# Borrowed homes for early weight splits, and half of a third group turned by VectorE

## The reference, cut to what matters

```
m = pool_conformer_mixer(rms(x, g), ...)    # stage 0: two matrices, depthwise convolution, pooling
x = x + rms(m, post_g)
x = x + rms(relu(rms(x, g) @ w1)**2 @ w2, post_g)      # stage 1: w1 2048 x 8192, w2 8192 x 2048
m = short_conv_mixer(rms(x, g), ...)        # stage 2: 2048 x 6144, a convolution of 3 taps, 2048 x 2048
x = x + rms(m, post_g)
x = x + rms(relu(rms(x, g) @ w1)**2 @ w2, post_g)      # stage 3: as stage 1
x = x + hybrid_layer(rms(x, g), ...)        # stage 4: attention, spatial gating, gates, output matrix
```

## Time and profile before

| | |
|---|---|
| median of 3 runs | 2675.39 us (2675.36 to 2675.88) |
| the profiled execution | 2675.7 us |
| its span | 2673.7 us |
| TensorE busy | 2668.5 us (100%) |
| VectorE busy | 1946.9 us (73%) |
| ScalarE busy | 1287.9 us (48%) |
| GpSimd busy | 286.2 us (11%) |
| mean DMA rate | 193 GB/s |
| the chain that ended last | TensorE 99% |

### The profile page before, as it was taken

One profiled execution on the slowest core, in us unless ns is written; L12 is line 12 of the kernel. 1 busy time (PEld: TensorE's weight loads), 2 busy tenths in 40 slices (PEclk: granted clock), 3 DMA queues, 4 the chain that ended last, 5 costly groups with the idle time before them and its releaser, 6 DMA issues.

```text
span 2673.7 us, 31093 instructions
## 1 busy us (share of the span) xinstructions
PE 2668.5 (100%) x11921; PEld 2210.5 (83%) x11921; DVE 1946.9 (73%) x2674; ACT 1287.9 (48%) x1625; POOL 286.2 (11%) x263
## 2 busy tenths in 40 slices
PE   9999999999999999999999999999999999999999
PEld 8888888888888888888888888888888888888887
DVE  6888867666766787776777676668668869985564
ACT  7775544444444454444544444344455545544442
POOL 4841100000000010000100000000011001000000
PEclk9999999999999999999999999999999999999999
DMA  7555655555655556555556655555555655565554
GB/s 258 188 173 190 210 199 189 189 189 190 207 186 191 202 185 210 192 199 193 187 190 205 204 188 183 196 189 193 192 184 188 212 174 175 177 215 189 189 189 157
DMA packets 268148, 515.57 MB, mean 193 GB/s; under 512 B 8498, under 2 KB 28260, under 8 KB 267492
## 3 DMA queue, kind: packets, MB, share of 16 engines
q1 hardware_dynamic: 267732, 513.34, 57.3%
q10 hardware_dynamic: 272, 0.26, 0.0%
HBM read 511.47 MB, written 2.10 MB: 192 GB/s over the span
## 4 chain that ended last, share of the span: by engine, by line
PE 99%; DVE 0%; DMA 0%; ACT 0%; issue 0%; SPq 0%; DVEq 0%; ACTq 0%
PE bank L833 32%; PE bank L835 32%; PE bank L834 32%; PE bank L884 0%; PE bank L901 0%; PE bank L1063 0%; DMA x_res<-in_x 0%; DVE w_lo L812 0%; DMA w_raw<-in_ab_w_in 0%; PE bank L1077 0%; DVE tap_product L2093 0%; DVE z L2081 0%; PE bank L1049 0%; PE bank L1086 0%; PE bank L1087 0%; PE bank L1024 0%
## 5 line engine op out<-in xcount | busy, mean ns | idle before, releaser
L812 DVE TENSOR_TENSOR w_lo<-w_raw,w_hi 128x1024 fp32r<-128x1024 f32 x950 | 1182.1, 1264 | 445.0 <-ACT w_hi L794 438.5
L794 ACT ACTIVATE w_hi<-w_raw 128x1024 fp32r<-128x1024 f32 x954 | 972.1, 1056 | 607.2 <-PE bank L835 415.8
L833 PE MATMUL bank<-w_hi,A_lo 128*128 128x512 f32 x2432 | 950.6, 391 | 0.1
L835 PE MATMUL bank<-w_hi,A_hi 128*128 128x512 f32 x2432 | 946.8, 389 | 0.0
L834 PE MATMUL bank<-w_lo,A_hi 128*128 128x512 f32 x2432 | 946.5, 389 | 0.0
L833 PE MATMUL bank<-w_hi,B_lo 128*128 128x512 f32 x1408 | 548.7, 390 | 0.0
L835 PE MATMUL bank<-w_hi,B_hi 128*128 128x512 f32 x1408 | 547.8, 389 | 0.0
L834 PE MATMUL bank<-w_lo,B_hi 128*128 128x512 f32 x1408 | 547.8, 389 | 0.0
L833 PEld LDWEIGHTS bank<-w_hi,A_lo 128*128 128x128 f32 x2432 | 456.6, 188 | 96.6 <-DVE w_lo L802 1.4
L835 PEld LDWEIGHTS bank<-w_hi,A_hi 128*128 128x128 f32 x2432 | 456.5, 188 | 95.3
L834 PEld LDWEIGHTS bank<-w_lo,A_hi 128*128 128x128 f32 x2432 | 456.7, 188 | 93.4
(11 more groups left out here) (181 smaller groups left out, 1020.9 us busy)
## 6 DMA issues: line engine op xcount, KB each, us to landing
w_raw<-in_ffn_w SPq DMA_DIRECT2D x256, 1024.0 KB, 5.2
w_raw<-in_w_in SPq DMA_DIRECT2D x88, 1024.0 KB, 5.0
w_raw<-in_sc_w_in SPq DMA_DIRECT2D x48, 1024.0 KB, 5.1
w_raw<-in_ab_w_out SPq DMA_DIRECT2D x16, 1024.0 KB, 5.0
w_raw<-in_sc_w_out SPq DMA_DIRECT2D x16, 1024.0 KB, 5.0
w_raw<-in_w_out SPq DMA_DIRECT2D x16, 1024.0 KB, 5.1
w_raw<-in_ab_w_in SPq DMA_DIRECT2D x26, 512.0 KB, 4.9
w_raw<-in_ab_w_in SPq DMA_DIRECT2D x8, 1024.0 KB, 5.1
```

The lines of the kernel that those rows point to most:

```text
L794: e.activation(w_hi[:, s % SPLIT_SLOTS, :], raw_step(s), ACT.Copy).then_inc(hi_made, 1)
L812: e.tensor_tensor(w_lo[:, slot, :], raw_step(s), w_hi[:, slot, :].bitcast(F32), ALU.subtract).then_inc(lo_made, 1)
L833: e.matmul(ps, lo[:, kt, tok], wh, start=first, stop=False)
L835: ins = e.matmul(ps, hi[:, kt, tok], wh, start=False, stop=last)
```

## The change

Four things change together.

1. **Homes.** The second and third step of the stages 1 to 4 (f+1, f+2, with f the stage's first step) have their split weights in groups 2 and 3 of A, `BORROWED`, in place of slots of `w_hi` and `w_lo`. The other steps go round the six slots without them. At the last yield of a stage the splitting goes on to f+2, and to f+3 at the start of the boundary. At the first steps it goes to f+7.
2. **Order of steps.** After the first four steps of both chunks come two of the first, two of the second, and so on, so group 3 is read from step +12 on.
3. **Turning.** TensorE turns only the first half of group 2 (four transposes). VectorE turns the second half with 16 transposes over four steps from +1 on, and group 3 over five steps from +5 on. The casts move: the second half of group 2 at steps (f+1 chunk, 1) and (f+1 chunk, 2), group 3 at (first chunk, 5) on ScalarE and (second chunk, 4) on VectorE.
4. **Small ones.** The step f+3 is no longer split in two halves. GpSimd's gain for the last chunk waits for the lower part of f+5. In stage 4 the turnings of the first two chunks begin after 3 and 6 steps and take 5 each.

```diff
-QK_TURNS = [(3, 6), (5, 6), (3, 5), (3, 5)]
+QK_TURNS = [(3, 5), (6, 5), (3, 5), (3, 5)]
...
             if first > 0:
-                for half in range(2):
-                    SEQ += [(c, 4 * half + i) for c in (first, first + 1) for i in range(4)]
+                SEQ += [(c, i) for c in (first, first + 1) for i in range(4)]
+                for half in range(2, 4):
+                    SEQ += [(c, 2 * half + i) for c in (first, first + 1) for i in range(2)]
...
+        BORROWED = {S0[STAGE[p]] + 1 + n: 2 + n for p in range(1, 5) for n in range(2)}
+        home, before_at, ring = [], [], []
+        for step in range(STEPS):
+            if step in BORROWED:
+                g = BORROWED[step]
+                home.append(tuple(v[:, GK * g:GK * g + GK, :].rearrange("p k t -> p (k t)") for v in halves["A"]))
+                before_at.append(None)
+            else:
+                home.append(tuple(v[:, len(ring) % SPLIT_SLOTS, :] for v in (w_hi, w_lo)))
+                before_at.append(ring[-SPLIT_SLOTS] if len(ring) >= SPLIT_SLOTS else None)
+                ring.append(step)
...
                 if stage > 0 and s < first + HELD:
-                    upto = min(upto, first + SPLIT_SLOTS - 1)
+                    upto = min(upto, first + SPLIT_SLOTS + 1)
+                upto = min(upto, end)
                 if s == end - HELD - 1:
-                    upto = end
-                split_to(e, one, at, min(upto, end))
+                    upto = end + EARLY_SPLITS - 1
+                split_to(e, one, at, upto)
...
+            def hi_half_turned(p):
+                e.wait_ge(half_turned.sem, half_turned.of(p))
+                for k in two:
+                    kt = GK * 2 + 2 + k
+                    ins = e.activation(halves["A"][0][:, kt, :], x_half_T[:, k, :], ACT.Copy, scale=par_col(PRE_COL[p], kt))
+                ins.then_inc(hi_cast("pre", p, 2, 1), 1)
...
             def hi_turned(p):
+                e.wait_ge(step_done, S0[STAGE[p]] + 3)
                 e.wait_ge(x_turned.sem, x_turned.of(p))
...
             def boundary(p):                               # ScalarE
                 f = S0[STAGE[p]]
+                split_to(e, split_hi, at, f + EARLY_SPLITS)
                 squares(p - 1, NG - 1, 0)
-                split_to(e, split_hi, at, f + 3)
+                split_to(e, split_hi, at, f + 5)
                 hi_tile(p, 0, 0)
                 hi_tile(p, 1, 0)
                 squares(p - 1, NG - 1, 1)
-                split_to(e, split_hi, at, f + 5)
+                split_to(e, split_hi, at, f + 6)
                 hi_tile(p, 0, 1)
                 hi_tile(p, 1, 1)
+                split_to(e, split_hi, at, f + 7)
 
             def early(p, c, i):
                 if (c, i) == (STAGE[p] + 1, 0):
-                    hi_x(p, 2)
+                    e.wait_ge(step_done, S0[STAGE[p]] + 2)
+                    hi_half(p, 2, 0)
                 if (c, i) == (STAGE[p] + 1, 1):
+                    hi_half_turned(p)
+                if (c, i) == (STAGE[p] + 1, 2):
                     statistics(p)
-                if (c, i) == (STAGE[p], 4):
+                if (c, i) == (STAGE[p], 5):
                     hi_turned(p)
...
             def boundary(p, alone=False):                  # VectorE
                 f = S0[STAGE[p]]
+                split_to(e, split_lo, at, f + EARLY_SPLITS)
                 finish(p - 1, NG - 1, 0, alone)
...
                 update(p - 1, 1, 0)
-                split_to(e, split_lo, at, f + 1)
+                split_to(e, split_lo, at, f + 4)
                 lo_tile(p, 0, 0)
-                split_to(e, split_lo, at, f + 2)
+                split_to(e, split_lo, at, f + 5)
                 finish(p - 1, NG - 1, 1, alone)
...
                 update(p - 1, 0, 1)
-                split_to(e, split_lo, at, f + 3)
+                split_to(e, split_lo, at, f + 6)
                 lo_tile(p, 0, 1)
...
                 lo_tile(p, 1, 1)
-                split_to(e, split_lo, at, f + 4)
+                split_to(e, split_lo, at, f + 7)
                 for tt in tiles:
                     update(p - 1, 3, tt)
-                split_to(e, split_lo, at, f + 5)
 
             def early(p, c, i):
+                n = POS[c, i] - S0[STAGE[p]] - 1
+                if 0 <= n < HALF_TURNS:
+                    turn_half(p, n)
                 if (c, i) == (STAGE[p] + 1, 0):
-                    lo_x(p, 2)
-                n = POS[c, i] - S0[STAGE[p]] - 3
-                if 0 <= n < 4:
+                    lo_half(p, 2, 0)
+                if (c, i) == (STAGE[p] + 1, 2):
+                    lo_half_turned(p)
+                n = POS[c, i] - S0[STAGE[p]] - 5
+                if 0 <= n < LAST_TURNS:
                     turn_last(p, n)
-                if (c, i) == (STAGE[p] + 1, 3):
+                if (c, i) == (STAGE[p] + 1, 4):
                     lo_turned(p)
-                if (c, i) == (STAGE[p], 4):
+                if (c, i) == (STAGE[p], 5):
                     statistics(p)
...
                 root(1, "postroot", "post", p, 0)             # GpSimd, finish
-                e.wait_ge(lo_made, S0[STAGE[p + 1]] + 3)
+                e.wait_ge(lo_made, S0[STAGE[p + 1]] + 6)
                 gain(p, NG - 1, 0)
```

More of the change, by code:

```diff
@@ L42 @@
 TURN_STEPS = 8
+HALF_TURNS = 4
+LAST_TURNS = 5
+EARLY_SPLITS = 3
 STEP_K = 2
@@ L241, in small_banks @@
     for key in turn_order():
-        if key[0] == "pre" and key[1] > 0 and key[2] == NG - 1:
+        if key[0] == "pre" and key[1] > 0 and (key[2] == NG - 1 or key[2:] == (2, 1)):
             continue
@@ L801, in split_lo_rows @@
                 e.wait_ge(hi_made, s + 1)
-            e.tensor_tensor(w_lo[:, slot, part], raw_step(s)[:, part], w_hi[:, slot, part].bitcast(F32),
+            e.tensor_tensor(home[s][1][:, part], raw_step(s)[:, part], home[s][0][:, part].bitcast(F32),
                             ALU.subtract).then_inc(half_lo(s) if k == 0 else lo_made, 1)
@@ L818, in step_matmuls @@
             hi, lo = halves[ch.buf]
-            slot, n = s % SPLIT_SLOTS, n_steps[c]
+            n = n_steps[c]
             for k in range(STEP_K):
@@ L827, in step_matmuls @@
                 kt = GK * ch.group0 + i * STEP_K + k
-                wh, wl = (v[:, slot, k * CH:(k + 1) * CH] for v in (w_hi, w_lo))
+                wh, wl = (v[:, k * CH:(k + 1) * CH] for v in home[s])
                 for tt in which:
@@ L875, in aux_begin, with turn @@
                 return aux_bank(*key)
-            def turn(src, *key):
-                for h in two:
+            def turn(src, *key, parts=two):
+                for h in parts:
                     view = aux_begin(*key, h).rearrange("p (k t) -> p k t", k=2)
@@ L891, in turn_x @@
                     e.wait_ge(x_made.sem, x_made.of(p - 1, g, 1))
-                turn(lambda tt, f: x[:, tt, g * CH + f.start:g * CH + f.stop], "pre", p, g)
+                turn(lambda tt, f: x[:, tt, g * CH + f.start:g * CH + f.stop], "pre", p, g,
+                     parts=range(1) if p > 0 else two)
             def turn_tile(p, g, tt):
@@ L1520, in lo_x, with turn_features, turn_half @@
                     lo_half(p, g, h)
+            def turn_features(dst, first, n_k, steps, n):
+                for m in range(16 * n // steps, 16 * (n + 1) // steps):
+                    tok, feat = (slice(32 * q, 32 * q + 32) for q in divmod(m, 4))
+                    ins = e.transpose(dst[feat, :, :].rearrange("p k (t c) -> p t k c", t=NT)[:, :, :, tok],
+                                      x[tok, :, first:first + n_k * P].rearrange("p t (k c) -> p t k c", k=n_k)[:, :, :, feat])
+                return ins
+            def turn_half(p, n):
+                if n == 0:
+                    e.wait_ge(x_made.sem, x_made.of(p - 1, 2, 1))
+                ins = turn_features(x_half_T, 2 * CH + CH // 2, 2, HALF_TURNS, n)
+                if n == HALF_TURNS - 1:
+                    ins.then_inc(half_turned(p), 1)
             def turn_last(p, n):
@@ L1525, in turn_last, with lo_half_turned @@
                     e.wait_ge(x_made.sem, x_made.of(p - 1, NG - 1, 1))
-                tok = slice(32 * n, 32 * n + 32)
-                for q in range(4):
-                    feat = slice(32 * q, 32 * q + 32)
-                    ins = e.transpose(x_T[feat, :, :].rearrange("p k (t c) -> p t k c", t=NT)[:, :, :, tok],
-                                      x[tok, :, D - CH:].rearrange("p t (k c) -> p t k c", k=GK)[:, :, :, feat])
-                if n == 3:
-                    ins.then_inc(x_turned(p), 1)
+                ins = turn_features(x_T, D - CH, GK, LAST_TURNS, n)
+                if n == LAST_TURNS - 1:
+                    ins.then_inc(x_turned(p), 1)
+            def lo_half_turned(p):
+                hi, lo = halves["A"]
+                e.wait_ge(hi_cast.sem, hi_cast.of("pre", p, 2, 1))
+                for k in two:
+                    kt = GK * 2 + 2 + k
```

(3 more changed lines are left out.)

17 lines of the change are left out of this document (9 added, 8 removed).

## The result

| | before | after |
|---|---|---|
| median | 2675.64 us (4 runs, 2675.36 to 2676.67) | 2715.02 us (4 runs, 2714.06 to 2715.40) |
| profiled execution, span | 2675.7, 2673.7 us | 2714.86, 2713.1 us |
| mean granted clock of TensorE | 1.000 | 0.994 |

The ratio is 1.0146 (95% interval 1.0134 to 1.0158): 39 us slower, where 23 were predicted, and outside the predicted range. The new code shifts the lines. VectorE's split, line 812 before, is now 829; ScalarE's, 794 before, is now 812; 901 is now 919, 1589 is 1641, 1611 is 1663, 1541 is 1593, 835 is 852.

What follows compares the result with a forecast made beforehand. TensorE, busy 2668.5 of 2673.7 us, was taken as the bound, so every wait is paid in full. Profiled 2675.7 - 1.7 + 14.2 + 10.8 (+23.3) gave 2699.0, as a median 2698.7 us; range 2685 to 2706.

Steps and rivals of the forecast that it cites:

- a rival with a chance of 0.14 and 2703 us: TensorE's clock falls in the new idle time at the boundaries, costing 2.8 us per wait less some 0.5; chance 0.14.
- 2717 if all eight: The clock rival's time if the clock falls at all eight boundary waits; 2701 if at the first alone.
- 16 transposes fewer: Four of eight TensorE transposes go at each of four boundaries, 0.44 us each time: -1.7 us.
- last evictions, TensorE's wait: At the boundaries, earlier splits await loads and squares, delaying the last eviction and x's update: 14.2 us, bounds 8 to 18.
- last group before +12: VectorE's half group and a wait for ScalarE's casts make TensorE wait 2.7 us before step +12: 10.8 us over four boundaries.
- stage 4's wait: Stage 4's moved turnings were costed at nothing; each transpose too many would cost 0.44 us if VectorE's room ran out.
- TensorE's idle time: Sign over the whole kernel: TensorE idle by some 24 us more in all.
- "against": Argument against the clock rival: the earlier trace's rows show a low clock nowhere behind a short wait.
- a margin that I had read away: At tile 0's turning, the update ending 943.84 was called just in time for TensorE's start at 943.93.
- The three rows of the mechanism: Before step +12: ScalarE's casts 1.61, f+13's upper part 1.09, VectorE's lower part 1.14 us in a row, adding 2.7.
- Edits costed at nothing: The first chunk's later end, stage 4's turnings and SyncE's sooner loads: 0 us; a load late by a microsecond costs one.
- The half group: VectorE's 16 added 32x128 transposes take 5.1 us per boundary (3.5 to 7.0), ahead of the last group's.

Runs made afterwards that it cites:

- kept-busy run: The changed kernel with unread identity transposes on TensorE before the first turning of each boundary and before each step +12: 2703.30 us (1.0103).
- twelfth experiment: The eleventh experiment with stage 4's first turning begun after 2 steps instead of 3: 2675.39 us (0.9999).
- fifth experiment: The third experiment with TensorE turning all of group 2 again at all four boundaries: 2677.84 us (1.0007).
- eleventh experiment: The eighth experiment with GpSimd's n=2 product for tile 0 ahead of the root, tile 1's only after VectorE's update of group 1, tile 0: 2675.09 us (0.9998).
- third experiment: The changed kernel with only f+1 split before the evictions, f+2 onward behind them, and f+13's upper part ahead of ScalarE's casts: 2690.66 us (1.0056).
- sixth: The third experiment with stage 4's second turning begun after 5 steps over 6, instead of after 6 over 5: 2689.45 us (1.0052).
- eighth experiment: The changed kernel with split and cast orders mended, group 3 turned in four steps, all of group 2 on TensorE at the first boundary: 2677.34 us (1.0006).

## Why the prediction was right and wrong

The direction and the places of all the boundary waits were right. The time was 16 us too low, and the step that failed is the clock: its fall in the waits stood in the sum with nothing and was left to a rival with a chance of 0.14 and 2703 us. The runs show the fall at seven of eight waits, worth 11.7 of the 16 us. The rival's own working held nearly the answer, "2717 if all eight", but in part by luck: it took 2.3 us per wait, where 1.7 were measured (11.7 in seven), and the other terms were 4.6 us too low.

| term | predicted | measured |
|---|---|---|
| 16 transposes fewer | -1.7 | 4 x -0.43 = -1.7 |
| last evictions, TensorE's wait | 6.2, 3.3, 1.6, 3.1 = 14.2 | 5.97, 4.49, 0.72 (+0.30), 3.40 = 14.9 |
| last group before +12 | 4 x 2.7 = 10.8 | 3.05, 3.04, 3.08, 3.04 = 12.2 |
| stage 4's wait | 0 | 1.3 |
| lower clock | 0 | 11.7 |
| sum | +23.3 | +38.4 of 39.2 |

The -0.43 is the time from the first transpose to the next matmul: 961.25 to 962.04 before, 978.90 to 979.26 after. TensorE's idle time (span less busy time) grew by 27.4 us, where the prediction said some 24 and its two terms add up to 25.0.

- **The clock.** I argued "against" from a trace that shows no low clock behind a short wait. But that trace has no such wait in mid-kernel, so it could say nothing. The only evidence was the start of the span, and that spoke for it. The kept-busy run shows the cost by itself. The Trainium skill, TensorE: Matmul & The Clock Gate, Part 1, says that an idle engine falls back to 1.2 GHz. The trace agrees, at waits of 3.04 us and more.
- **Last evictions.** They are late by 6.4, 5.2, 1.4 and 4.15 us, 17.1 for 14.2. At the second boundary the load of f+2 landed a microsecond later than carried over from the earlier trace rows, 6.6 for 5.6. Why isn't traced: the loads ahead of it and the next one are issued at the same distances as before, and over the runs this load takes 5.6 to 7.1. At the first boundary it landed sooner, 7.0 for 7.7. And at three boundaries the split of f+3 took 2.14, 2.17 and 2.18 us for 1.22, beside GpSimd's products (the third has none there: 1.22). What made up for it is a margin that I had read away: TensorE turns as soon as the first of the two updates is done, 942.42 + 0.71 = 943.13, and it was busy till 943.93. I had set the end of both (943.84) against it. That is 0.7 to 0.8 us at every boundary: 5.2 late, 4.5 waited. (At the first, 6.4 and 5.97, half of it is used up: the small operation ahead of the root comes 0.33 later behind the eviction than before.) Two errors of opposite sign, so that 14.9 came out near 14.2 is in part luck.
- **Last group.** The 32x128 transposes take 0.302 us by the groups of VectorE, 5.04 for 16, against 0.31 to 0.32 and 5.1:
```profile
L1558 DVE STREAM_TRANSPOSE conv_out<-x_res 32x128 f32<-32x128 f32 x64 | 19.3, 302 | 0.8
```
  The wait is 3.05 for 2.7. The three rows of the mechanism (casts 996.59, upper part 998.21, lower part 999.28) stand as predicted. The 0.35 left over isn't traced to one row.
- **Edits costed at nothing.** SyncE's loads and the first chunk's end cost nothing that a wait shows. Stage 4 did cost 1.3 us: "busy shares leave VectorE room" is an average over the kernel. In that stretch VectorE has 1.23 us of split and 1.34 of transposes in a step of 2.73, and a reduction and two products beside them. How much of the wait is due to the turnings' new places is open: with the second one a step earlier 0.85 to 1.0 stay, and the kernel before is as full there, as the twelfth experiment shows.
- **The half group.** That it has no room on VectorE ahead of +12 in this order was right, and the fifth experiment shows it alone: 12.8 us less with the half on TensorE. The rule in the Trainium skill, VectorE: DVE Perf Modes, Rules for kernel authors, to turn 128x128 on TensorE, agrees here. The eleventh experiment turns the half on VectorE at three boundaries and is level with the kernel before, so it is a question of room on VectorE.

## What to carry to other kernels

Where a change makes a busy TensorE wait for some microseconds, price the lower clock behind the wait with the wait itself: here 11.7 us on top of 28.4. A trace in which it never waits is no evidence against that. When work is moved ahead of a deadline, count what is left between that deadline and the next, in both directions: three splits moved back cost 3.1 us at the next one. And look at what GpSimd does beside a VectorE instruction that a chain depends on, before using VectorE's pause.

## What the runs showed of the hardware

- **The clock falls in a wait or just behind it.** With TensorE idle from 955.7 to 960.0 the granted clock is 1.00 in 956 to 960 and 0.59 in 960 to 964; with it idle from 244.1 to 249.9 it is 0.50 from 247.4 on. It fell at all seven waits of 3.04 us and more, and not at one of 0.72. In the third experiment, with waits of 2.4 us at the four boundaries, it fell at two of them (14 slow matmuls), in the sixth, with the same waits, at all four (28). Identity transposes in the waits kept it full.
- **VectorE and GpSimd shut each other out.** A split takes 2.17 us and not 1.22 beside a product of GpSimd, GpSimd's pair 3.24 and not 2.54 beside a split, the update pair 3.45 and not 1.42, and a 128x1 operation 1.13 and not 0.16. Where one meets one, the later is held up till the earlier is done: GpSimd's pair ends at 955.85, and the split issued at 954.77 ends 1.09 after that, about its own duration. The evictions, which read PSUM and one operand in SBUF, aren't slower: 0.69 in the eighth experiment at 940.89, while GpSimd's pair runs. SBUF — State Buffer in the Trainium skill, Who interferes with whom, says that a VectorE instruction with two SBUF inputs contends with a GpSimd instruction that reads SBUF, and that the second to issue blocks until the first is done. The traces agree, with the numbers above. By that rule the collision could have been foreseen: 0.95 us at three boundaries.
